# Attention: scores of two units of a couple of heads made together, the odd unit's in the second banks

## What is computed

```python
for i in range(S // Q_BLOCK):                       # Q_BLOCK = 128, S = 1024
    q0, q1 = i * Q_BLOCK, (i + 1) * Q_BLOCK
    qb = q[:, :, q0:q1]
    kp, vp, cp = k[:, :, :q1], v[:, :, :q1], c[:, :, :q1]
    s = jnp.einsum('bhqd,bhkd->bhqk', qb, kp).astype(jnp.float32) * scale
    s = s + c[:, :, q0:q1, None] - cp[:, :, None, :]
    mask = (q0 + jnp.arange(Q_BLOCK))[:, None] >= jnp.arange(q1)[None, :]
    s = jnp.where(mask[None, None], s, -1e30)
    p = jax.nn.softmax(s, axis=-1).astype(v.dtype)
    outs.append(jnp.einsum('bhqk,bhkd->bhqd', p, vp))
```

## Time and profile before

| | us |
|---|---|
| median of 3 runs | 1433.44 |
| lowest, highest | 1433.23, 1434.01 |
| the profiled execution | 1432.45 |
| its span | 1430.3 |

### The profile page before, as it was taken

How to read it: one execution, slowest core, us unless ns; L and a number is a source line. 1 busy time by engine, 2 the same in 40 slices (tenths; PEclk the granted TensorE clock), 3 DMA queues, 4 the chain that set the end, 5 groups by cost and what they waited for, 6 DMA issues and landing times.

```text
span 1430.3 us, 19604 instructions
## 1 busy us (share of the span) xinstructions
PE 1408.4 (98%) x7122; PEld 1153.8 (81%) x7122; DVE 993.4 (69%) x1442; ACT 630.1 (44%) x1196; POOL 550.9 (39%) x571
## 2 busy tenths in 40 slices
PE   8999999999999999999999999999999999999998
PEld 5878888887677788888888788888888888888886
DVE  7846495546867737877657877776777767785867
ACT  6545343334866644556444532233322332444445
POOL 5733243334545312013013654454444443354402
PEclk9999999999999999999999999999999999999999
DMA  8264264445322298314203112333332335883334
GB/s 214 53 127 114 58 135 102 73 82 200 118 97 77 73 285 197 106 60 133 60 0 147 64 58 95 110 111 111 110 109 87 106 111 205 302 284 99 89 104 148
DMA packets 107145, 172.14 MB, mean 120 GB/s; under 512 B 7293, under 2 KB 63121, under 8 KB 105514
## 3 DMA queue, kind: packets, MB, share of 16 engines
q1 hardware_dynamic: 98016, 146.59, 34.3%
q0 software_dynamic: 5408, 15.76, 4.3%
q10 hardware_dynamic: 3626, 8.54, 1.6%
HBM read 125.42 MB, written 42.30 MB: 117 GB/s over the span
## 4 chain that ended last, share of the span: by engine, by line
PE 89%; ACT 3%; POOL 3%; DVE 2%; issue 1%; DMA 1%; DVEq 0%; ACTq 0%; POOLq 0%
PE ps L2326 27%; PE ps L2328 27%; PE ps L2327 27%; PE ps L2526 2%; PE ps L2535 2%; PE ps L2558 1%; ACT prob L1324 1%; DMA w_raw<-in_w_xkv 1%; ACT prob_t L1315 1%; PE ps L2388 1%; PE ps L2696 0%; POOL tok_f L920 0%; POOL w_lo L871 0%; POOL x_t L911 0%; DVE hf_lo_B L1618 0%
## 5 line engine op out<-in xcount | busy, mean ns | idle before, releaser
L2326 PE MATMUL ps<-t_lo,s_hi 128*128 128x512 f32 x308 | 119.9, 389 | 0.1
L2328 PE MATMUL ps<-t_hi,s_lo 128*128 128x512 f32 x308 | 119.8, 389 | 0.0
L2327 PE MATMUL ps<-t_hi,s_hi 128*128 128x512 f32 x308 | 119.8, 389 | 0.0
L2326 PE MATMUL ps<-h_lo_T,w_hi 128*128 128x512 f32 x256 | 100.6, 393 | 1.8 <-ACT u_t L1235 1.0
L1618 DVE TENSOR_TENSOR s_lo<-w_raw,s_hi 128x512 fp32r<-128x512 f32 x77 | 62.4, 810 | 56.8 <-ACT s_hi L1533 56.7
L1533 ACT ACTIVATE s_hi<-w_raw 128x512 fp32r<-128x512 f32 x77 | 48.7, 632 | 118.0 <-PE ps L2328 91.8
L2328 PE MATMUL ps<-h_hi_T,w_lo 128*128 128x512 f32 x256 | 99.7, 389 | 0.0
L2327 PE MATMUL ps<-h_hi_T,w_hi 128*128 128x512 f32 x256 | 99.6, 389 | 0.0
L1549 ACT ACTIVATE p_sb<-ps 128x512 f32<-128x512 f32 x22 | 13.1, 598 | 187.5 <-PE ps L2328 187.5
L2326 PE MATMUL ps<-hf_lo_T,w_hi 128*128 128x512 f32 x212 | 82.5, 389 | 0.0
L2327 PE MATMUL ps<-hf_hi_T,w_hi 128*128 128x512 f32 x212 | 82.5, 389 | 0.0
(11 more groups left out here) (402 smaller groups left out, 4318.9 us busy)
## 6 DMA issues: line engine op xcount, KB each, us to landing
w_raw<-hs_dram SPq DMA_DIRECT2D x77, 256.0 KB, 2.7
raw_p<-in_w_ffn_in SPq DMA_DIRECT2D x22, 512.0 KB, 4.6
w_raw<-in_w_ffn_in SPq DMA_DIRECT2D x22, 512.0 KB, 4.3
hs_dram<-h_sum SPq DMA_DIRECT2D x11, 1024.0 KB, 8.9
hs_dram<-hq SPq DMA_DIRECT2D x11, 768.0 KB, 7.1
wq_B<-in_w_ffn_out SPq DMA_DIRECT2D x8, 1024.0 KB, 7.8
raw_f<-in_w_in SPq DMA_DIRECT2D x14, 512.0 KB, 7.1
gate_dram<-c_st SPq DMA_DIRECT2D x28, 256.0 KB, 2.0
```

The costliest lines, as they stand in the source:

```text
L2326: nc.tensor.matmul(dst, w_h, x_l, start=start, stop=False, skip_group_check=onto)
L2327: nc.tensor.matmul(dst, w_h, x_h, start=False, stop=False, skip_group_check=onto)
L2328: return nc.tensor.matmul(dst, w_l, x_h, start=False, stop=stop, skip_group_check=onto)
```

## The change

`scores_in(u)` says whose scores step u makes. In couples 0, 2 and 3 the even steps with i = 0 and 2 make those of units u and u + 1, one after the other, and the steps with i = 1 and 3 make none and drop their wait for `sc_biased` at that place. Couple 1 and all units with i >= 4 stay as they are. `score_bank(u)` puts the scores of units with i = 1 and 3 of these couples into the second bank of each head (1 and 3 in place of 0 and 2), and DVE's biasing reads them there. Nothing else moves.

```diff
+def scores_in(u):
+
+    if u == PAIRS * T:
+        return ()
+    if u // T != 1 and u % T < 4:
+        return () if u % 2 else (u, u + 1)
+    return (u,)
+
+
+def score_bank(u):
+
+    return 1 if u // T != 1 and u % T in (1, 3) else 0
@@
-                b, n = u % 2, (i + 1) * P
+                b, n, s0 = u % 2, (i + 1) * P, score_bank(u) * HALF
@@
-                    nc.vector.tensor_tensor_reduce(out=prob[b][:, a, 0:n], in0=two(2 * a)[:, 0:n], in1=negc[h % 3][:, 0:n],
+                    nc.vector.tensor_tensor_reduce(out=prob[b][:, a, 0:n], in0=two(2 * a)[:, s0:s0 + n], in1=negc[h % 3][:, 0:n],
@@
+            def scores_of(u):
+
+                p, i = divmod(u, T)
+                for c in range(0, i + 1, 4):
+                    n = min(4, i + 1 - c)
+                    keys = slice(c * P, (c + n) * P)
+                    for term, (q, k) in enumerate(((q_lo, k_hi), (q_hi, k_hi), (q_hi, k_lo))):
+                        for a in range(2):
+                            head = slice(a * DH, (a + 1) * DH)
+                            last = nc.tensor.matmul(ps[:, 2 * a + c // 4 + score_bank(u), 0:n * P], q[p % 2][head, tile_of(i)],
+                                                    k[p % 2][head, keys], start=term == 0, stop=term == 2)
+                            if term == 2 and c + n == i + 1:
+                                last.then_inc(sc_done, 1)
@@
-                if u < PAIRS * T:
+                if scores_in(u):
                     pe.wait_ge(qk_lo, 4 * p + 4)
                     if u == 12:
                         pe.wait_ge(mix_lo, 7)
                     if u:
                         pe.wait_ge(sc_biased, 2 * u)
-                    for c in range(0, i + 1, 4):
...
-                                    last.then_inc(sc_done, 1)
+                    for e in scores_in(u):
+                        scores_of(e)
```

## The result

The changed kernel takes 1435.75 us (median of 17 runs, 1433.96 to 1437.03) against 1433.23 for the kernel before on the same chip (17 runs, 1431.79 to 1434.01). The medians are 2.5 us apart; the ratio is 1.0016, 95% interval 1.0010 to 1.0022, or 1.4 to 3.2 us. The forecast was 1435.4, or +2.0.

The account below looks back on a forecast made before the run. The prediction took PE, busy 98% of the span, as the bound. Couple 0 +0.70, couple 2 +0.82 and couple 3 +0.48 summed to +2.0 us, giving 1435.4 from the three runs' median 1433.44; 8-in-10 range 1432.2 to 1437.3.

Parts of the forecast that it names:

- A: The forecast itself: merges delay even steps, odd steps give back only part; 1435.4 us, chance 0.54.
- the price of 256 columns: Scores put in at units 1, 17 and 25: half the 512-wide price per group, 0.36 us in all.
- the wait before unit 20: PE waits some 0.4 us before unit 20's scores for unit 19's biasing, late behind `q_lo`.
- units 0/1: Couple 0: the inserted 0.36 us is hidden, since the next fill waits for a DVE step anyway; 0.
- units 2/3: Couple 0: unit 3's scores delay a loop through PE, ACT and DVE by their full length; +0.70 us.
- units 16/17: Couple 2: the inserted scores delay ACT's copies of transposes, nothing recovered in step 17; +0.36 us.
- units 18/19 with unit 20's wait: Couple 2: gating limits what step 19 recovers, and unit 19's late biasing holds unit 20's scores; +0.46 us.
- units 24/25: Couple 3: as at units 16 and 17, ACT's copies come later and nothing is recovered; +0.36 us.
- units 26/27: Couple 3: 0.70 us put in, 0.58 given back before the fill waits for gating; +0.12 us.
- Closed loop: Unit 1's transposes, ACT's copies, unit 2's exp, normalisation and transposes form one chain, starting 0.70 us later.
- The alternative that `q_lo` starts before POOL: Couple 2: unit 19's biasing would be ready early, couple 2 end at +0.48 and the sum at +1.7 us (1435.1).
- B: Rival: only PE's queue counts, each merge saves changes between fills and scores; 1.56 us off, 1431.9, chance 0.12.

Follow-up runs that it names:

- half_b: Changed kernel with only units 0/1, 18/19 and 24/25 merged, the others as in the kernel before; 1432.85 us, one run.
- half_a: Changed kernel with only units 2/3, 16/17 and 26/27 merged, the others as in the kernel before; 1435.27 us, one run.
- late: Against the changed kernel: only 2/3, 18/19 and 26/27 paired, the odd unit's scores placed after the even step's first transposes; 1433.90 us, ratio 1.0006.
- short_gate: Changed kernel with DVE's gating of products 4 and 11 cut to 64 of 512 columns, the rest zeroed; 1436.02 us, one run.
- low19: Changed kernel with POOL's fourth `w_lo` moved from after step 18 to after step 19; 1435.41 us, one run.
- early11m: early11s with one of the three low parts of the mixing left in step 10, ahead of unit 11's biasing; 1431.31 us, ratio 0.9984.
- early11: Kernel before, with DVE's low parts of the mixing and of `q` moved behind unit 11's biasing; 1432.03 us, ratio 0.9994.
- early11s: early11 with PE's wait for the low parts moved from unit 12's first scores to its second group; 1431.81 us, ratio 0.9990.
- after_early11: Changed kernel with early11's edit added; 1434.26 us, ratio 1.0007 against the kernel before.
- longer: Kernel before, with one more DVE instruction of `q_lo`'s kind ahead of unit 11's biasing; 1434.32 us, ratio 1.0005.

## Why the prediction came out

It was right in sign and mechanism, and near in size: 1435.4 forecast, 1435.75 measured, inside A's own range of 1434.6 to 1436.0. Two terms were sized too small, the price of 256 columns and the wait before unit 20. In the order of its steps:

| term | forecast, us | measured, us | from |
|---|---|---|---|
| units 0/1 | 0 | 0.09 | half_b |
| units 2/3 | 0.70 | 0.70 | half_a |
| units 16/17 | 0.36 | 0.41 | half_a |
| units 18/19 with unit 20's wait | 0.46 | 0.53 | half_b |
| units 24/25 | 0.36 | 0.38 | half_b |
| units 26/27 | 0.12 | 0.15 | half_a |
| sum | 2.00 | 2.26 | |

- **Units 0/1.** The fill at 340.74 was held not to move against its chain. Measured from unit 0's scores it moves by 0.06 in half_b (340.33 less 336.91, before 340.74 less 337.38), and unit 2's scores by the 0.09. The cover was thin: the prediction left 0.04 (339.87 to 339.91) between the delayed fill and the DVE step, and the price below uses that up. In half_b the fill ends at 339.46 and the DVE step starts at 339.49, which is 0.05 later than before, counted from unit 0's scores. The last 0.03 of the 0.09 lies in the fills behind, without a wait.
- **Units 2/3.** Closed loop, exact, and the idle time of about 1 us before unit 2's transposes is 1.09. late shows the reason, by taking the scores out from in front of the loop.
- **The price of 256 columns.** This was one mis-sized term. Half of 0.235 for each of three terms gave 0.36, but the first term after other scores takes 0.17 (337.29 to 337.46) and only the others 0.12. From unit 0's first scores to the next fill are 0.48 us before (337.38 to 337.86) and 0.89 after (336.90 to 337.79), so 0.41 goes in, 0.05 more at each of 0/1, 16/17 and 24/25 (of which 24/25 ended at 0.38).
- **Units 16/17.** Nothing is recovered, as reckoned: the wait of 0.34 for ACT's copies stands where the scores had been (no run takes this wait away, so it rests on the rows), and the next fill starts 1.86 after the transposes (421.88 to 423.74), as before (419.66 to 421.52, 1.86).
- **Units 18/19 and 26/27.** The fill waits for gating with 1.26 us from the last fill (431.88 to 433.14; forecast 1.27). PE's own way was put at 0.92 and is 0.23 + 0.63 = 0.86 or less; short_gate shows 0.24 + 0.57 = 0.81. The sum did not use it, since gating ends last.
- **Unit 20.** The wait is 0.37 (forecast about 0.4), released by L1920, and low19 takes 0.41 off the stretch. This was the other mis-sized term. The prediction let PE start 0.06 after the biasing (434.51 to 434.57), though it had itself read 0.15 for such a release, and 0.15 it is (436.35 to 436.50). Of the 0.30 that the biasing had to spare, only 0.15 was cover. With 0.15 couple 2 comes to +0.91, and with 0.05 for the price to +0.96, where 0.95 was measured; in half_b it is 0.70 less 0.15, measured 0.53. The alternative that `q_lo` starts before POOL did not happen: `w_lo` started 0.72 earlier.
- **Base.** The profiled execution of before was of the lower group of its runs, and the three given runs of the upper one. Adding the sum to the median of the three rather than to the profiled time was right, since both groups exist in both kernels. That 0.35 us is all that separates 1435.4 from 1435.75 owes something to luck: both medians lie in the upper group because 10 of 17 runs fell there each time, and two runs fewer in one of them would have moved its median by 0.6 to 1.0 us.

The sum was 0.3 low against the stretches (2.27) and 0.5 low against the medians (2.52). What is beyond 2.27 lies within the interval of the ratio (1.4 to 3.2 us). B counted 1.56 us of saved changes of kind; in the odd steps they became waits of PE for ACT or DVE.

The Trainium skill, page Perfetto Trace Analysis, section Optimizing Tensor Performance, advises to rotate independent groups of matmuls through different banks. Here the second banks bought nothing. PE's waits for biasing before the change, which are its waits for banks of scores, stand before units 6 (0.27 us) and 12 (2.04 us), whose scores the change leaves where they were; no row shows one before a unit that was moved. The earlier place in the queue cost 2.3 us (the stretches).

## What to carry to other kernels

On an engine that works in order, making something earlier means making everything behind it later: before a product is moved forward, follow the chain that starts at the next instruction behind it, and ask whether the slot it leaves has work that is ready. Scores beside another engine's chain are free where they are, and can cost their full length in front of it. And look first at the longest single wait: here a few DVE steps moved behind one biasing, with the wait that they met (early11m), gained 2.3 us by the medians (1.0 to 3.6 by the interval of the ratio), as much as the studied change lost.

## What was not expected of the hardware

- **The clock after 2 us of idle time.** With 2.04 us idle before unit 12's scores, the granted clock of PE around the end of it fell to 0.50 (1.2 GHz level) for some 3 us in some executions, and stayed at 1.00 (2.4 GHz) in others. The fall need not come while PE is idle: in half_a PE goes on at 390.76, and it falls after 391.50 (the windows below). It makes units 12 to 16 take 24.0 in place of 22.5 us, and splits the runs into two groups some 1.4 to 1.7 us apart (upper group: 10 of 17, before and after). With 1.35 us idle (early11, early11s, after_early11) or 0.27 (early11m) one run of 44 stood apart (early11's at 1433.51); with 2.64, 8 of 11 were in the upper group. In every profiled execution with the low clock in this stretch (after, half_a, low19, short_gate, longer) PE had idled 2.04 us or more before it, and in others with 2.04 us (before, half_b, late) it stayed high. What decides it there stays open; early11 changed both the length and the place of the idle time.

```profile
391.00:391.50 0.50, 0.50 (x6) 0.48 (x6) 0.47 (x2) 0.50 (x3) 0.42 (x2) 1.00 0.59 221
391.50:392.00 0.50, 0.50 (x8) 0.48 (x5) 0.44 (x3) 0.50 (x2) 0.50 (x2) 0.57 0.01 4
```

- **Idle time shown is less than what a wait costs.** 0.22 us stood in the row and 0.47 went away with the wait (short_gate): the idle time counts from the end shown of the matmul before, and matmuls overlap in these rows (transposes 0.82 long, the next fill 0.57 after their start). Starts are to be compared.
- **Changes of kind between matmuls are not free.** Scores put between transposes and a fill took 1.07 us where the scores themselves take 0.70 (late), so placing them where no chain waits still cost 0.51 in couples 2 and 3.
